# Feed-forward stages of a two-block transformer kernel: one PSUM operand for VectorE's operations of a turn, and the root applied to the up side when it is split

## The chip, the cores and the metric

The kernel runs on one core of a Trainium2 chip. The metric is the device time of one execution in microseconds. Engine names in the profile: PE is TensorE (PEld its weight loads), DVE is VectorE, ACT is ScalarE, POOL is GpSimd, SP is SyncE, which issues the DMAs of the weights.

## The reference, cut to what matters

The program is two blocks of a transformer on 512 tokens of width 1024, in float32. Each block ends in a feed-forward part of hidden width 2816. In the first block:

```python
u = rms_norm(h, norm_ffn_g[l])
g, up = jnp.split(u @ w_gate_up[l], 2, axis=-1)
h = h + (jax.nn.silu(g) * up) @ w_down[l]
```

The second block has the same with other names. `rms_norm` multiplies by `rsqrt(mean(h*h) + 1e-6)`, one number per token, and by a gain. Since that number (the root, `rs` in the kernel) is the same for all columns of a token, the kernel multiplies h by the gain only ahead of the product, and by rs behind it. With G and U for the two products without rs, the hidden value is

```
a = silu(G*rs) * (U*rs) = G*rs * sigmoid(G*rs) * U*rs
```

so rs is applied once ahead of the sigmoid and appears twice in the product.

## The kernel before

**Precision.** TensorE multiplies in a rounded format. Each operand is therefore kept as a high part (a rounded copy, made by ScalarE) and a low part (the operand minus its high part), and each product is three matmuls: high by high, high by low, low by high. The low parts of the weights (`w_lo`, `low_part`, L501) are made by GpSimd, each one a subtraction of 128x1024 elements whose two inputs are in SBUF.

**Weights.** All weights come in one stream of units of 128x1024, in a ring of three slots. For each unit SyncE issues the load, ScalarE makes w_hi (`feed`, L1392) once the load has landed and TensorE is done with the unit three before it, whose slot it takes, GpSimd makes w_lo, and TensorE uses it. SyncE may reload a slot when its w_lo is done.

**The feed-forward stages.** ffn1 and ffn2 have 44 units each, gate and up tiles by turns. Tokens lie along the free dimension, so a hidden tile is 128 (columns) x 512 (tokens). The first units (6 in ffn1, 12 in ffn2) and the last two are plain: one unit is one tile of 24 matmuls (`tile_unit`). Between them are turns of six units (6 turns in ffn1, 5 in ffn2, `fast_turns` and `turn`). In a turn the first two pairs of units (e=0 and e=1) are each computed with seven half products of 12 matmuls in place of eight (Strassen's scheme as Winograd orders it; `seven_products`), and the last two units are plain tiles. The scheme needs sums of the weights: VectorE makes three tiles `s_raw` from a pair of units (`weight_sums`, L2631 to L2634), ScalarE the high part `s_hi` (L1810), GpSimd the low part `s_lo` (L521). `weight_sums(i, 1)` serves pair e=1 of the turn, `weight_sums(i, 3)` pair e=0 of the next turn. It needs similar sums of u (`t_sums`, L2601 to L2607, and `t_low`, L2614), which are made once at the stage's head.

**What VectorE does per turn**, in this order (`ffn_dve`, `turn`): the up tile of the turn before (`plain_up`, L2583); the weight sums of pair 1; `late_sums` (L2641), after which it signals `fast_z`, on which TensorE waits ahead of the pair's seventh product; `late_up` (L2646); `fast_gate` (L2652 to L2657), which completes the gate tile and multiplies it by rs into tmp[1]; ScalarE's sigmoid E of it goes to PSUM bank 3; `fast_up` (L2665 to L2667): E times gate, times rs, times up, into `a_raw`. The same for e=1, with the weight sums of pair 3 ahead of its `fast_up`. Then the plain gate tile (`plain_gate`, L2569), whose sigmoid goes to `e_tmp` in SBUF, and `plain_mid` (L2577, L2578): gate times E, times rs. `step` makes VectorE wait for each operation's own end before the next.

**The order is written out by hand** on each engine; nothing is planned. Each engine works through its program in order, and semaphores tie them.

**The end of a stage.** The high parts a_hi lie where the sums of u and weights were (t_hi, t_lo, s_raw), and a_lo is written in the place of a_raw. So they can be made only behind the last product of the last turn. ScalarE's `split(k)` makes a_hi from a_raw when `fast_a` says tile k is done; VectorE's `split` makes a_lo behind it (L2674). Between them the last gate and up tiles are done. ScalarE feeds the last unit of ffn and the first two of the down stage among its splits; the down stage's third unit and those behind it are fed by `down_act`, behind all 22 splits and a load of the activation table, and in ffn1 also behind the eight squares of `mem_in` (L1412, L1417). From the third on, each of those waits for VectorE's addition (`add_square`, L2194), and these stand behind VectorE's last split. `down` on TensorE (banks 2 to 5 first, then 6, 7, 0, 1) uses two hidden tiles per unit.

Of the kernel before, what the change touches and what calls it, by code (L numbers as in the profile page):

```python
# [116 lines left out]
def build(nc, stream, xT, memT, vecs, tabs, relb, outT):  # L117
    with ExitStack() as ctx, ExitStack() as work:
# [89 lines left out]
        t_raw = [ar(f"t_raw{i}", [P, 4, HALF], F32, 80 + 4 * i) for i in range(2)]  # L208
        first_two = tmp[2]
        late_two = tmp[4]  # L210
        e_tmp = tmp[5]

        bq = ar("bq", [P, 4, T], F32, 0)
        bk = ar("bk", [P, 4, T], F32, 8)
# [102 lines left out]
        def named(n):  # L317
            if n not in nsem:
                nsem[n] = sem(n)
            return nsem[n]  # L320
# [70 lines left out]
        def ffn2_banks(pair):  # L391

            return [(1, 6), (0, 7), (4, 5)][pair]

        FAST = {"ffn1": (FIRST["ffn1"] + 2 * R, 6), "ffn2": (FIRST["ffn2"] + 4 * R, 5)}
        E_BANK = 3

        def out_banks(pair):

# [977 lines left out]
        def _(act):  # L1377
# [398 lines left out]
            def ffn_act(name, first, at_end=None):  # L1776
# [3 lines left out]
                if name == "ffn1":  # L1780
                    act.sem_inc(named("fast_s_used"), 2)

                def gate(dst):

                    gates.use()
                    act.wait_ge(*of_fast(name, "gate", gates.value()))
                    act.activation(dst, tmp[1][:, :], ACT.Sigmoid).then_inc(named("fast_e"), 1)

                def plain_gate():
                    gate(e_tmp[:, :])  # L1790

                def t_tile(k):

# [25 lines left out]
                def split(k):  # L1819

                    act.wait_ge(*of_fast(name, "a", k + 1))
                    act.activation(a_hi[:, k], a_raw[:, k], ACT.Copy).then_inc(named("raw_hi"), 1)

                def turn(i, last):

                    feed_at(i, 2)
                    copy(i, 0)
                    sums_hi(i, 1)
                    feed_at(i, 3)
                    feed_at(i, 4)  # L1830
                    gate(ps[:, E_BANK, :])
                    copy(i, 1)
                    feed_at(i, 5)
                    feed_at(i, 6)
                    gate(ps[:, E_BANK, :])
                    if last:
                        act.wait_ge(*of_fast(name, "s_used", 2 * turns + 2))
                        if at_end:
                            at_end()
                        for k in range(4):  # L1840
                            split(k)
                        feed_at(i, 7)
                        plain_gate()
                        for k in range(4, 8):
                            split(k)
                        feed_at(i, 8)
                        for k in range(8, 12):
                            split(k)
                        feed_at(i, 9)
                        plain_gate()  # L1850
                        for k in range(12, 20):
                            split(k)
                    else:
                        sums_hi(i, 3)
                        feed_at(i, 7)
                        plain_gate()

                first(FIRST[name], plain_gate, t_tile, sums_hi)
                with repeat(act, turns - 1, [(gates, R)]) as i:
                    turn(i, False)  # L1860
                turn(turns - 1, True)
                split(20)
                split(21)
                exponentials()

            def memory_split():
# [314 lines left out]
        def _(dve):  # L2181
# [374 lines left out]
            def ffn_dve(name, gain):  # L2556
# [13 lines left out]
                    dve.sem_inc(bank_free[bank], 1)  # L2570
                    dve.sem_inc(named("fast_gate"), 1)

                def plain_mid():

                    made.use()
                    dve.wait_ge(*of_fast(name, "e", made.value()))
                    step(dve.tensor_tensor(tmp[1][:, :], tmp[1][:, :], e_tmp[:, :], ALU.mult))  # L2577
                    step(dve.tensor_tensor(tmp[1][:, :], tmp[1][:, :], rs[:, :], ALU.mult))  # L2578

                def plain_up(t, bank, k):  # L2580

                    dve.wait_ge(w_used, t + 1)
                    step(dve.tensor_tensor(a_raw[:, bass.ds(k, 1)], ps[:, bank, :].unsqueeze(1), tmp[1][:, :].unsqueeze(1),  # L2583
                                           ALU.mult))
                    dve.sem_inc(bank_free[bank], 1)
                    dve.sem_inc(named("fast_a"), 1)

                def pair(j, banks):

# [47 lines left out]
                def late_sums(i, e):  # L2637

                    dve.wait_ge(*of_fast(name, "prod", i * 4 + (2 * e + 2)))
                    dve.wait_ge(*of_fast(name, "copied", i * 2 + (e + 1)))  # L2640
                    step(dve.tensor_tensor(late_two[:, :], ps[:, ffn2_banks(e)[1], :], first_two[:, :], ALU.add))  # L2641
                    dve.sem_inc(named("fast_z"), 1)

                def late_up():

                    step(dve.tensor_tensor(late_two[:, H], late_two[:, H], late_two[:, L], ALU.add))  # L2646

                def fast_gate(i, e):

                    x, y = ffn2_banks(e)  # L2650
                    dve.wait_ge(*of_fast(name, "s_used", i * 2 + (e + 3)))
                    step(dve.tensor_tensor(tmp[1][:, H], ps[:, y, H], late_two[:, L], ALU.add))  # L2652
                    dve.sem_inc(bank_free[y], 1)
                    step(dve.tensor_tensor(tmp[1][:, L], ps[:, x, L], rs[:, L], ALU.mult))
                    step(dve.tensor_tensor(tmp[1][:, H], tmp[1][:, H], rs[:, H], ALU.mult))  # L2655
                    dve.sem_inc(named("fast_gate"), 1)
                    step(dve.tensor_tensor(late_two[:, L], ps[:, x, H], late_two[:, L], ALU.add))  # L2657
                    dve.sem_inc(bank_free[x], 1)

                def fast_up(k):  # L2660

                    made.use()
                    dve.wait_ge(*of_fast(name, "e", made.value()))
                    x = ps[:, E_BANK, :]
                    step(dve.tensor_tensor(x, x, tmp[1][:, :], ALU.mult))  # L2665
                    step(dve.tensor_tensor(x, x, rs[:, :], ALU.mult))
                    step(dve.tensor_tensor(a_raw[:, bass.ds(k, 1)], x.unsqueeze(1), late_two[:, :].unsqueeze(1), ALU.mult))  # L2667
                    dve.sem_inc(named("fast_a"), 1)

                def split(first, last):  # L2670

                    for k in range(first, last):
                        dve.wait_ge(*of_fast(name, "a_hi", k + 1))
                        step(dve.tensor_tensor(a_lo[:, k], a_raw[:, k], a_hi[:, k].bitcast(F32), ALU.subtract))  # L2674
                        dve.sem_inc(named("raw_lo"), 1)

                def turn(i, last):

# [32 lines left out]
                plain_gate(u - 2, ffn2_banks(2)[0])  # L2711
                plain_mid()

                with repeat(dve, turns - 1, [(own, 30), (made, 3)]) as i:
                    turn(i, False)
                turn(turns - 1, True)
                t = u + turns * 2 * R
                split(0, 2)
                plain_up(t - 1, ffn2_banks(2)[1], FT - 2)
                split(2, 6)  # L2720
                plain_gate(t, ffn2_banks(0)[0])
                split(6, 10)
                plain_mid()
                plain_up(t + 1, ffn2_banks(0)[1], FT - 1)
                split(10, FT)

            def down_ready(name, n):
                if n < 3:
# [451 lines left out]
```

## Time and profile before

| | |
|---|---|
| time, median of 3 runs | 1761.22 us (1760.53 to 1762.3) |
| the profiled execution's own time | 1761.26 us |
| its span (first to last instruction) | 1759.4 us |
| mean granted TensorE clock | 0.99 |
| busy, share of the span | TensorE 96%, VectorE 58%, GpSimd 43%, ScalarE 42% |

The span is 1.9 us shorter than the execution's own time. In the profile a line such as L737 is a line of the kernel before; a group is one line with one kind of operands. "tmp<-ps,tmp" is an operation that writes a tile in SBUF from one in PSUM (ps) and one in SBUF. In brackets stands the engine's idle time ahead of the operation and what ended it; "x2" are two operations in a row shown as one. The clock is a share of full speed. In time, ffn1's turns run from about 442 to 645 us, ffn2's from about 1442 to 1607.

### The profile page before, as it was taken

Reading aid. Unit: us, or ns where it says so; the run is one execution under the profiler, and the core shown is the slowest. Engines: PE = TensorE matmul, PEld = TensorE weight load, DVE = VectorE, ACT = ScalarE, POOL = GpSimd, SP = SyncE. Lnnn points to the kernel's source line nnn. Section 1 sums busy time; section 2 is a strip of 40 time slices with the busy share of each in tenths; the row PEclk is TensorE's granted clock in tenths of the full one; section 3 lists DMA queues with packets and bytes.
Section 4 is the critical chain, followed back from the end, with each engine's and each line's share of the span. In section 5 each row is a group of like instructions: output and inputs, shape, how many; then the busy total and the mean of one; then the engine's idle time right before and its main releaser. Section 6 shows DMA issues by size and latency. Waiting matters only on the chain.

```text
span 1759.4 us, 25747 instructions
## 1 busy us (share of the span) xinstructions
PE 1693.7 (96%) x8873; PEld 1393.2 (79%) x8877; DVE 1017.9 (58%) x1608; ACT 731.9 (42%) x1187; POOL 757.9 (43%) x330
## 2 busy tenths in 40 slices
PE   9999999999889997999999999999999988999999
PEld 7888777787788886888788766778888868888887
DVE  6744875657776674207497676642324886677413
ACT  7333554433333343326434576552233523334322
POOL 2444222444666663354433102544444336656443
PEclk9999999999999998999999999999999989999999
DMA  5444221232222332234422111223323212333332
GB/s 198 130 147 140 95 61 49 84 91 78 85 85 92 97 119 72 82 110 122 145 88 93 41 45 48 61 65 93 105 92 113 72 60 84 97 94 96 96 96 72
DMA packets 47643, 162.37 MB, mean 92 GB/s; under 512 B 5724, under 2 KB 7900, under 8 KB 47304
## 3 DMA queue, kind: packets, MB, share of 16 engines
q1 hardware_dynamic: 43440, 150.70, 27.6%
q10 hardware_dynamic: 4120, 10.59, 1.9%
q8 instruction: 48, 0.79, 0.2%
q14 instruction: 35, 0.29, 0.1%
HBM read 156.91 MB, written 4.76 MB: 92 GB/s over the span
## 4 chain that ended last, share of the span: by engine, by line
PE 73%; DVE 17%; issue 4%; ACT 3%; POOL 2%; DVEq 1%; ACTq 0%; POOLq 0%
PE ps L619 18%; PE ps L621 17%; PE ps L620 17%; DVE tmp L2578 2%; PE ps L737 2%; PE ps L739 2%; PE ps L738 2%; PE ps L877 2%; POOL s_lo L521 2%; PE ps L859 2%; DVE tmp L2577 2%; DVE s_raw L2631 1%; DVE tmp L2655 1%; PE ps L1311 1%; PE ps L1310 1%
## 5 line engine op out<-in xcount | busy, mean ns | idle before, releaser
L501 POOL TENSOR_TENSOR w_lo<-w_raw,w_hi 128x1024 fp32r<-128x1024 f32 x260 | 642.6, 2480 | 764.2 <-ACT w_hi L1392 737.4
L1392 ACT ACTIVATE w_hi<-w_raw 128x1024 fp32r<-128x1024 f32 x271 | 284.1, 1054 | 333.2 <-PE ps L621 223.0
L619 PE MATMUL ps<-u_hi,w_hi 128*128 128x512 f32 x984 | 404.0, 411 | 11.3 <-POOL w_lo L501 11.1
L621 PE MATMUL ps<-u_hi,w_lo 128*128 128x512 f32 x984 | 385.1, 391 | 0.0
L620 PE MATMUL ps<-u_lo,w_hi 128*128 128x512 f32 x984 | 385.0, 391 | 0.0
L619 PEld LDWEIGHTS ps<-u_hi,w_hi 128*128 128x128 f32 x984 | 185.6, 189 | 57.0 <-POOL w_lo L501 12.2
L621 PEld LDWEIGHTS ps<-u_hi,w_lo 128*128 128x128 f32 x984 | 185.4, 188 | 40.0
L620 PEld LDWEIGHTS ps<-u_lo,w_hi 128*128 128x128 f32 x984 | 185.9, 189 | 37.0 <-issue 1.4
L521 POOL TENSOR_TENSOR s_lo<-s_raw,s_hi 128x1536 fp32r<-128x1536 f32 x22 | 77.0, 3500 | 112.8 <-ACT s_hi L1810 112.8
L619 PE MATMUL ps<-a_hi,w_hi 128*128 (+1 forms) x264 | 104.1, 394 | 9.7 <-POOL w_lo L501 9.7
L620 PE MATMUL ps<-a_lo,w_hi 128*128 (+1 forms) x264 | 103.7, 393 | 0.0
L621 PE MATMUL ps<-a_hi,w_lo 128*128 (+1 forms) x264 | 103.5, 392 | 0.0
L1810 ACT ACTIVATE s_hi<-s_raw 128x1536 fp32r<-128x1536 f32 x22 | 32.7, 1488 | 108.7 <-DVEq L2635 108.7
L568 POOL TENSOR_TENSOR masked_bias<-bias,pick 128x128 f32<-128x128 f32 (+3 forms) x32 | 25.5, 824 | 104.5 <-PE ps L1207 103.7
L737 PE MATMUL ps<-t_hi,s_hi 128*128 128x256 f32 x176 | 52.4, 298 | 16.0 <-POOL s_lo L521 16.0
L619 PEld LDWEIGHTS ps<-a_hi,w_hi 128*128 128x128 f32 x264 | 50.1, 190 | 20.5 <-issue 10.1
L2533 DVE TENSOR_TENSOR tmp<-ps,tmp 128x512 f32<-128x512 f32 x16 | 11.1, 691 | 91.1 <-PE ps L621 90.0
L621 PEld LDWEIGHTS ps<-a_hi,w_lo 128*128 128x128 f32 x264 | 50.1, 190 | 10.7
L620 PEld LDWEIGHTS ps<-a_lo,w_hi 128*128 128x128 f32 x264 | 50.1, 190 | 10.5
L619 PE MATMUL ps<-m_hi,w_hi 128*128 128x512 f32 (+1 forms) x152 | 54.3, 357 | 0.0
L620 PE MATMUL ps<-m_lo,w_hi 128*128 128x512 f32 (+1 forms) x152 | 54.0, 356 | 0.0
L621 PE MATMUL ps<-m_hi,w_lo 128*128 128x512 f32 (+1 forms) x152 | 54.0, 356 | 0.0
(456 smaller groups left out, 3647.5 us busy)
## 6 DMA issues: line engine op xcount, KB each, us to landing
w_raw<-stream SPq DMA_DIRECT2D x277, 512.0 KB, 3.5
g_rep<-g_one ACTq DMA_DIRECT2D x1, 2560.0 KB, 13.1
spread<-m_rows ACTq DMA_DIRECT2D x4, 512.0 KB, 4.2
tmp<-tmp ACTq DMA_DIRECT2D x32, 64.0 KB, 3.1
bias<-g_rep ACTq DMA_DIRECT2D x1, 2048.0 KB, 10.6
outT<-hT SPq DMA_DIRECT2D x13, 128.0 KB, 1.8
hT<-xT SPq DMA_DIRECT2D x3, 512.0 KB, 7.4
mem_in<-memT ACTq DMA_DIRECT2D x1, 1024.0 KB, 6.4
```

Source lines behind the costliest of these rows:

```text
L501: pool.tensor_tensor(w_lo[:, slot], w_raw[:, slot], w_hi[:, slot].bitcast(F32), ALU.subtract)\
L521: pool.tensor_tensor(s_lo[pair % 3][:, :, :], s_raw[:, :, :], s_hi[pair % 3][:, :, :].bitcast(F32), ALU.subtract).then_inc(named("raw_lo"), 1)
L619: pe.matmul(out, wh, xh, start=start, stop=False)
L620: pe.matmul(out, wh, xl, start=False, stop=False)
L621: return pe.matmul(out, wl, xh, start=False, stop=stop)
L737: pe.matmul(out, w_h(k), x_h(k), start=start and k == 0, stop=False, skip_group_check=True)
L738: pe.matmul(out, w_h(k), x_l(k), start=False, stop=False, skip_group_check=True)
L739: m = pe.matmul(out, w_l(k), x_h(k), start=False, stop=stop and k == HK - 1, skip_group_check=True)
L859: m = pe.matmul(ps[:, 2 + e, 0:keys[t]], head_q(h, t), head_k(h, keys[t]), start=True, stop=not extra(t))
L877: m = pe.matmul(ps[p0:p1, b, t * P:t * P + P], values(h, kb), prT[e][:, kb * P:kb * P + P], start=kb == 0, stop=kb == nb - 1)
L1392: act.activation(w_hi[:, slot], w_raw[:, slot], ACT.Copy).then_inc(hi_ready, 1)
L2577: step(dve.tensor_tensor(tmp[1][:, :], tmp[1][:, :], e_tmp[:, :], ALU.mult))
```

## The change

Four things change, all in ffn1 and ffn2.

1. **The root of the up side.** `fast_up` and `plain_mid` no longer multiply by rs. `a_raw` is therefore without the second rs, and a new step `rooted` multiplies each of its 22 tiles by rs in place, behind the last turn and ahead of the split. The signal `fast_a`, on which ScalarE's `split` waits, moves from `fast_up` and `plain_up` to `rooted`.
2. **E in PSUM.** The sigmoid of the plain gates goes to PSUM bank 3 as those of the other gates do, the very last one to bank 7; `e_tmp` goes. `plain_mid` is one multiply that reads E from PSUM.
3. **Sums through bank 2.** `late_sums` is split in two halves, one of which goes to bank 2; `fast_gate` puts its half-wide sum in bank 2 in place of tmp[1]. So `late_up` and the multiply of old line 2655 read one operand from PSUM.
4. **The order of the end.** VectorE roots tiles 0 and 1, then 2 to 5, 6 to 9, with the splits a group behind, then root k and split k-2 by turns up to the last. ScalarE has its feeds and gates among the splits in another spacing: feed, gate, splits 0 and 1, feed, splits 2 to 5, feed, gate, splits 6 to 21.

```diff
-        e_tmp = tmp[5]
-        E_BANK = 3
+        C_BANK, E_BANK, LAST_E_BANK = 2, 3, 7
...
-                def gate(dst):
+                def gate(bank=E_BANK):
...
-                    act.activation(dst, tmp[1][:, :], ACT.Sigmoid).then_inc(named("fast_e"), 1)
+                    act.activation(ps[:, bank, :], tmp[1][:, :], ACT.Sigmoid).then_inc(named("fast_e"), 1)
...
                     if last:
                         act.wait_ge(*of_fast(name, "s_used", 2 * turns + 2))
                         if at_end:
                             at_end()
-                        for k in range(4):
-                            split(k)
                         feed_at(i, 7)
-                        plain_gate()
-                        for k in range(4, 8):
+                        gate()
+                        for k in range(2):
                             split(k)
                         feed_at(i, 8)
-                        for k in range(8, 12):
+                        for k in range(2, 6):
                             split(k)
                         feed_at(i, 9)
-                        plain_gate()
-                        for k in range(12, 20):
+                        gate(LAST_E_BANK)
+                        for k in range(6, FT):
                             split(k)
...
-                def plain_mid():
+                def plain_mid(bank=E_BANK):
...
-                    step(dve.tensor_tensor(tmp[1][:, :], tmp[1][:, :], e_tmp[:, :], ALU.mult))
-                    step(dve.tensor_tensor(tmp[1][:, :], tmp[1][:, :], rs[:, :], ALU.mult))
+                    step(dve.tensor_tensor(tmp[1][:, :], ps[:, bank, :], tmp[1][:, :], ALU.mult))
...
-                    step(dve.tensor_tensor(late_two[:, :], ps[:, ffn2_banks(e)[1], :], first_two[:, :], ALU.add))
+                    y = ffn2_banks(e)[1]
+                    step(dve.tensor_tensor(late_two[:, L], ps[:, y, L], first_two[:, L], ALU.add))
+                    step(dve.tensor_tensor(ps[:, C_BANK, H], ps[:, y, H], first_two[:, H], ALU.add))
...
-                    step(dve.tensor_tensor(late_two[:, H], late_two[:, H], late_two[:, L], ALU.add))
+                    step(dve.tensor_tensor(late_two[:, H], ps[:, C_BANK, H], late_two[:, L], ALU.add))
...
-                    step(dve.tensor_tensor(tmp[1][:, H], ps[:, y, H], late_two[:, L], ALU.add))
+                    step(dve.tensor_tensor(ps[:, C_BANK, L], ps[:, y, H], late_two[:, L], ALU.add))
...
-                    step(dve.tensor_tensor(tmp[1][:, H], tmp[1][:, H], rs[:, H], ALU.mult))
+                    step(dve.tensor_tensor(tmp[1][:, H], ps[:, C_BANK, L], rs[:, H], ALU.mult))
...
-                    step(dve.tensor_tensor(x, x, rs[:, :], ALU.mult))
                     step(dve.tensor_tensor(a_raw[:, bass.ds(k, 1)], x.unsqueeze(1), late_two[:, :].unsqueeze(1), ALU.mult))
-                    dve.sem_inc(named("fast_a"), 1)
...
+                def rooted(first, last):
+
+                    for k in range(first, last):
+                        step(dve.tensor_tensor(a_raw[:, k], a_raw[:, k], rs[:, :], ALU.mult))
+                        dve.sem_inc(named("fast_a"), 1)
...
-                split(0, 2)
+                rooted(0, 2)
                 plain_up(t - 1, ffn2_banks(2)[1], FT - 2)
-                split(2, 6)
+                rooted(2, 6)
+                split(0, 4)
                 plain_gate(t, ffn2_banks(0)[0])
-                split(6, 10)
-                plain_mid()
+                rooted(6, 10)
+                plain_mid(LAST_E_BANK)
+                split(4, 8)
                 plain_up(t + 1, ffn2_banks(0)[1], FT - 1)
-                split(10, FT)
+                for k in range(10, FT):
+                    rooted(k, k + 1)
+                    split(k - 2, k - 1)
+                split(FT - 2, FT)
```

## Rows read from the trace of the kernel before

**Rows 1.** The page's busy line: busy us, share of the span, instructions per engine.
```profile
PE 1693.7 (96%) x8873; PEld 1393.2 (79%) x8877; DVE 1017.9 (58%) x1608; ACT 731.9 (42%) x1187; POOL 757.9 (43%) x330
```

**Rows 2.** What TensorE waited for, whole span: total us, times, longest.
```profile
PE ps L619 <- POOL w_lo L501: 20.8, 3, 9.7
...
PE ps L737 <- DVEq L2642: 20.0, 11, 2.0
...
PE ps L737 <- POOL s_lo L521: 16.0, 18, 5.2
```

**Rows 3.** TensorE in time order, ffn1: start, us, line, operation [idle before].
```profile
496.15 0.39 PE L737 MATMUL ps<-t_hi,s_hi 128*128 128x256 f32 x1 [1.10 <-POOL s_lo L521]
...
504.89 0.40 PE L619 MATMUL ps<-u_hi,w_hi 128*128 128x512 f32 x1
...
527.03 0.39 PE L737 MATMUL ps<-u_hi,s_hi 128*128 128x256 f32 x1 [1.96 <-DVEq L2642]
...
531.27 0.39 PE L737 MATMUL ps<-t_hi,s_hi 128*128 128x256 f32 x1 [1.10 <-POOL s_lo L521]
```

**Rows 4.** VectorE's groups by line and shape: busy us, mean ns, idle before.
```profile
L2578 DVE TENSOR_TENSOR tmp<-tmp,tmp 128x512 f32<-128x512 f32 x22 | 42.4, 1927 | 0.8
...
L2655 DVE TENSOR_TENSOR tmp<-tmp,tmp 128x256 f32<-128x256 f32 x22 | 41.1, 1870 | 0.8
...
L2666 DVE TENSOR_TENSOR ps<-ps,tmp 128x512 f32<-128x512 f32 x22 | 15.4, 700 | 0.8
```

**Rows 5.** VectorE in time order, the same turn of ffn1.
```profile
505.09 0.42 DVE L2652 TENSOR_TENSOR tmp<-ps,tmp 128x256 f32<-128x256 f32 x1 [2.96 <-PE ps L739]
505.66 0.42 DVE L2654 TENSOR_TENSOR tmp<-ps,tmp 128x256 f32<-128x256 f32 x1
506.12 2.28 DVE L2655 TENSOR_TENSOR tmp<-tmp,tmp 128x256 f32<-128x256 f32 x1
...
509.35 0.69 DVE L2631 TENSOR_TENSOR s_raw<-w_raw 128x512 f32<-128x512 f32 x1 [0.38 <-DVE tmp L2657]
...
516.50 1.61 DVE L2577 TENSOR_TENSOR tmp<-tmp,tmp 128x512 f32<-128x512 f32 x1 [0.85 <-ACT tmp L1787]
518.14 2.78 DVE L2578 TENSOR_TENSOR tmp<-tmp,tmp 128x512 f32<-128x512 f32 x1
...
521.60 0.69 DVE L2583 TENSOR_TENSOR a_raw<-ps,tmp 128x512 f32 x1 [0.67 <-DVE tmp L2578]
522.79 0.95 DVE L2631 TENSOR_TENSOR s_raw<-w_raw 128x512 f32<-128x512 f32 x1 [0.50 <-DVE a_raw L2583]
```

**Rows 6.** GpSimd in time order, the same turn.
```profile
503.35 4.77 POOL L501 TENSOR_TENSOR w_lo<-w_raw,w_hi 128x1024 fp32r<-128x1024 f32 x2 [2.34 <-ACT w_hi L1392]
...
514.04 3.52 POOL L521 TENSOR_TENSOR s_lo<-s_raw,s_hi 128x1536 fp32r<-128x1536 f32 x1 [5.93 <-ACT s_hi L1810]
...
517.50 5.69 POOL L501 TENSOR_TENSOR w_lo<-w_raw,w_hi 128x1024 fp32r<-128x1024 f32 x2
```

**Rows 7.** End of ffn1: VectorE's last turn and last splits, TensorE's wait.
```profile
645.59 0.42 DVE L2652 TENSOR_TENSOR tmp<-ps,tmp 128x256 f32<-128x256 f32 x1 [3.13 <-PE ps L739]
...
671.16 9.93 DVE L2674 TENSOR_TENSOR a_lo<-a_raw,a_hi 128x512 fp32r<-128x512 f32 x12 [0.25 <-DVE a_raw L2583]
...
687.83 0.79 PE L619 MATMUL ps<-a_hi,w_hi 128*128 x1 [9.69 <-POOL w_lo L501]
```

**Rows 8.** End of ffn2: VectorE's last raw tile, GpSimd's first w_lo behind it.
```profile
1632.01 0.69 DVE L2583 TENSOR_TENSOR a_raw<-ps,tmp 128x512 f32<-128x512 f32 x1
...
1635.98 2.45 POOL L501 TENSOR_TENSOR w_lo<-w_raw,w_hi 128x1024 fp32r<-128x1024 f32 x1 [8.64 <-ACT w_hi L1392]
```

**Rows 9.** Heads of ffn1 and ffn2: TensorE's waits in time order.
```profile
447.43 0.58 PE L737 MATMUL ps<-t_hi,s_hi 128*128 128x256 f32 x1 [5.25 <-POOL s_lo L521]
...
1434.18 0.79 PE L619 MATMUL ps<-u_hi,w_hi 128*128 128x512 f32 x1 [8.38 <-POOL w_lo L501]
```

**Rows 10.** Busy time and granted clock in the window behind ffn1's wait.
```profile
688.00:692.00 4.00, 4.00 (x10) 3.13 (x11) 0.00 (x0) 0.00 (x0) 4.00 (x2) 0.50 0.57 156
```

More of the change, by code:

```diff
@@ L1781, in ffn_act @@
                     act.sem_inc(named("fast_s_used"), 2)
-                def gate(dst):
+                def gate(bank=E_BANK):
                     gates.use()
                     act.wait_ge(*of_fast(name, "gate", gates.value()))
-                    act.activation(dst, tmp[1][:, :], ACT.Sigmoid).then_inc(named("fast_e"), 1)
-                def plain_gate():
-                    gate(e_tmp[:, :])
+                    act.activation(ps[:, bank, :], tmp[1][:, :], ACT.Sigmoid).then_inc(named("fast_e"), 1)
                 def t_tile(k):
@@ L1830, in turn @@
                     feed_at(i, 4)
-                    gate(ps[:, E_BANK, :])
+                    gate()
                     copy(i, 1)
@@ L1834, in turn @@
                     feed_at(i, 6)
-                    gate(ps[:, E_BANK, :])
+                    gate()
                     if last:
@@ L1839, in turn @@
                             at_end()
-                        for k in range(4):
-                            split(k)
                         feed_at(i, 7)
-                        plain_gate()
-                        for k in range(4, 8):
+                        gate()
+                        for k in range(2):
                             split(k)
                         feed_at(i, 8)
-                        for k in range(8, 12):
+                        for k in range(2, 6):
                             split(k)
                         feed_at(i, 9)
-                        plain_gate()
-                        for k in range(12, 20):
+                        gate(LAST_E_BANK)
+                        for k in range(6, FT):
                             split(k)
@@ L1855, in turn @@
                         feed_at(i, 7)
-                        plain_gate()
-                first(FIRST[name], plain_gate, t_tile, sums_hi)
+                        gate()
+                first(FIRST[name], gate, t_tile, sums_hi)
                 with repeat(act, turns - 1, [(gates, R)]) as i:
@@ L1861, in ffn_act @@
                 turn(turns - 1, True)
-                split(20)
-                split(21)
                 exponentials()
@@ L2665, in fast_up @@
                     step(dve.tensor_tensor(x, x, tmp[1][:, :], ALU.mult))
-                    step(dve.tensor_tensor(x, x, rs[:, :], ALU.mult))
                     step(dve.tensor_tensor(a_raw[:, bass.ds(k, 1)], x.unsqueeze(1), late_two[:, :].unsqueeze(1), ALU.mult))
-                    dve.sem_inc(named("fast_a"), 1)
                 def split(first, last):
@@ L2712, in ffn_dve @@
                 plain_mid()
-                with repeat(dve, turns - 1, [(own, 30), (made, 3)]) as i:
+                with repeat(dve, turns - 1, [(own, 29), (made, 3)]) as i:
                     turn(i, False)
```

## The prediction

> **What bounds the kernel now.** I read the page's busy line first, then TensorE's waits, the lines with their shapes, one turn of ffn1 in time order, and last the ends of the stages. TensorE is busy 1693.7 of 1759.4 us [rows 1], so only 65.7 us of idle can be won. Three rows hold 56.8 of them [rows 2]: 20.8 us for a w_lo (three waits), 20.0 for VectorE's `fast_z` (L2642), 16.0 for the s_lo of a weight sum. The last two, both on L737, come back in each of the eleven turns of ffn1 and ffn2: 1.96 and 1.10 us in one turn [rows 3], and 0.23 more for the s_lo of its first sum. The turn lasts 35.12 us (531.27 less the 496.15 of the same product one turn earlier).
>
> VectorE is late in a turn because some of its operations are stretched. With both inputs in SBUF the 512-wide L2578 takes 1927 ns on average and the 256-wide L2655 1870; L2666 (512), which reads PSUM, takes 700 [rows 4], and L2652 (256) 0.42 us. In the turn, L2655 (506.12 to 508.40) can only have worked in its last 0.42 us, from 507.98: GpSimd's pair of w_lo ends at 508.12 [rows 5, 6]. L2577 (its last 0.69 begins at 517.42) comes through as the s_lo ends (517.56), L2578 waits for the first w_lo of the next pair (to 520.23) and L2631 for the second (to 523.05, pair's end 523.19). So a VectorE operation with two SBUF inputs waits for the GpSimd operation under way, until 0.14 us before its recorded end, and then the engines alternate: 0.69 for VectorE, 2.12 for a w_lo.
>
> The Trainium skill ("SBUF — State Buffer", Who interferes with whom) says the same of two SBUF inputs against a GpSimd operation that reads SBUF: whoever issues first holds the port for the whole instruction, the other fully blocks. It speaks against this change in the ends below, whose added operations all have two SBUF inputs. Held for the recorded length, each collision would cost 0.14 us more, about 3 us in the sum; the rows decide for the shorter one.
>
> **A full turn after the change.** I count x from the turn's first plain tile (504.89 [rows 3]). TensorE does two tiles to x=10.92, then products of 1.44 (12 matmuls, 0.12 between starts). VectorE starts at x=0.20.
> Pair 3: L2655 reads PSUM, 0.43 instead of 2.28. L2657 ends at 2.24; the weight sums would start at 2.62 (0.38 gap, as before 509.35), wait for the w_lo pair until 3.1 and end at 5.95 (0.69+3×0.72), before at 7.33. Their s_lo is ready at 11.3; TensorE wants it at 12.36. The wait of 0.23 goes.
> `fast_up` loses L2666 (0.73); the gate L2569 ends at 8.6, the sigmoid at 9.5, the middle multiply (one, from PSUM) at 10.2, where L2578 ended at 16.03. What is late next is TensorE: the up tile ends at 10.92, so L2583 runs 11.3 to 12.0 instead of 16.71 to 17.40 [rows 5].
> Pair 1: its sums could start at 12.5 (0.50 gap), and they keep two SBUF inputs. Behind s_lo GpSimd has two w_lo in a row, 11.25 to 13.5 and on (the second one's w_hi waits for the up tile too, ready at 12.2). L2631 waits to 13.5 and ends at 14.2, L2632 waits to 16.3, the four end at 18.45 (before: 21.02).
> `fast_z`: L2641, now two of 0.43, is done at 19.65. TensorE wants it at 10.92+6×1.44=19.56: 0.2 of the 1.96 stays.
> s_lo of pair 1 comes 5.36 after its sums (from 522.79+0.95+3×0.725 = 525.91 to 531.27 before), 23.8; TensorE, 0.3 late, wants it at 22.75: 1.05 of the 1.10 stays. Six more products: 23.9+8.64=32.55. **A full turn takes 32.55 instead of 35.12, 2.55 us less, nine times (five in ffn1, four in ffn2): 22.9.** That is more than the idle shown, since a stop costs 0.26 beyond it: a matmul's modelled end lies 0.16 behind the next start, and the first one behind a stop takes 0.39, not 0.28.
> In the first turn of each stage both stay late, since its sums of pair 1 meet the same two w_lo: 1.1 less each, 2.2.
>
> **The heads.** ffn1: L2578 (2.85 at one pair, 2.83 at the next) goes; 1.2 is lost again, as the t-sums wait for the w_lo of 421.14 instead, and 1.1 as L2631 meets one. The first product with a sum starts 3.4 earlier than 447.43 [rows 9]. ffn2: four pairs lose 0.72 each ahead of the feed that ends the 8.38 wait of 1434.18 [rows 9], and collisions of its t-sums shift: 2.6 (bounds 0 and 5). Together 6.0.
> Won: 22.9+2.2+6.0 = 31.1 us.
>
> **The ends.** Here work is added: 22 multiplies by rs (`rooted`) per stage behind the last turn, each ahead of ScalarE's a_hi of its tile. No row shows them; the nearest is two SBUF inputs, 512 wide, GpSimd quiet: 0.69 (the last three sums of a turn), plus 0.15 for the increment behind it (L2652 to L2654 in [rows 5] shows that gap): 0.84. A split costs 0.845 likewise.
> I count D from L2652 of the last turn (645.59 [rows 7]). The gate waits for its tile to 5.5; middle done 7.8; root 0 waits for a w_lo, root 1 done 10.4; up waits for its tile (x=11.1, which is D 10.9), done 11.7; root 2 12.55; a w_lo holds root 3 to 14.65; root 5 17.0; splits 0 to 3 with one w_lo 22.5; gate 23.3; roots 6 to 9 26.7; middle 27.55; splits 4 to 7 30.9; up 31.75; then twelve times root and split, 1.69 each. The last root ends at 31.95+11×1.69+0.69 = 51.2, the last split at 53.8, before at 35.5 (681.09, [rows 7]). a_lo itself isn't late: splits 0 and 1 are done at 18.8, down's first unit starts at 21.8; 2 and 3 at 22.5, the second at 27.2.
> What TensorE will lack is weights. ScalarE feeds down's third unit only behind its last `split`, and in ffn1 behind the squares of mem_in too, whose additions stand behind VectorE's last split. TensorE wants that unit at 687.83-9.69-645.59 = D 32.55 [rows 7].
> ffn1: the chain from last split to w_lo is the same, so all of it moves by 53.8-35.5: **18.3**; the 9.69 wait becomes 28.
> ffn2 has no squares. From its last raw tile (1632.70) over a_hi, table load, w_hi and w_lo (to 1635.98+2.4 [rows 8]) are 5.7: 51.2+5.7 = 56.9 against 32.55: **24.4**, where no wait stood. Behind such a wait the granted clock is 0.50, 1.2 GHz [rows 10]; ffn1's end has that already, in ffn2's twelve matmuls are new at 0.43 between starts instead of 0.23: 2.4.
> Nothing gives this back: TensorE has no other long wait in [rows 2] behind either end.
> Cost: 18.3+24.4+2.4 = 45.1. Bounds: with no w_lo in VectorE's way each end is 4.1 shorter, 36.9 in all; with roots at L2578's 1.93 it would be 94, but GpSimd is idle through most of the tail for want of feeds, so I stay near the lower bound. The turn's term lies between 0 and 3.97 (no stop left, 31.15).
>
> **Sum:** 45.1-31.1 = +14.0 us on the profiled execution's 1761.26 (span 1759.4 and 1.9 around it): 1775.3. The median of the runs shown is 1761.22, the same within their spread.
>
> At nothing I put: E in PSUM at plain gates (ScalarE writes beside VectorE's next wait), bank 7 for the last E (free until down's second half), `late_up` and `fast_gate` through bank 2 (same widths, no other user of bank 2 in a turn). Uncovered, they'd cost under 0.1 a turn. No DMA is added; SP's loads follow w_lo and the sums, and at the ends they have long landed when ScalarE comes.
>
> **Rivals.**
> (a) Not slower: VectorE gets the port twice running when a w_lo ends. Then L2631 and L2632 pass together, s_lo comes 2 us earlier, and a turn has no stop. Won 9×3.97+4+6.7 = 46.4; at the ends roots aren't held, 36.9: **1751.8**. If the turns alone have it, **1760.0**. It decides from 4 us won a turn. For: at 509 to 512 four operations follow one another freely; against: L2578 lost the port right behind L2577.
> (b) GpSimd keeps the port through both w_lo: the sums of pair 1 end 0.5 later, turn 33.1, won 2.0 instead of 2.55: **1780**. Against: L2577 got in between.
> (c) It doesn't do what it says, PSUM readers wait too: no gain, 45 lost: **1806**. Against: L2652 and L2654 took 0.42 inside a w_lo.
>
> **Numbers.** Forecast 0.50; (a) in full 0.10, in the turns alone 0.17; (b) 0.20; (c) 0.03. Faster by over 0.2% (3.5 us, about what can be told from no change here): 0.11; within: 0.16; slower: 0.73. The range 1757 to 1781 takes in (b) and (a) in the turns.
>
> **What would show it.** L2655 and the middle multiply at 0.43 and 0.69; turns of 32.6 with a fast_z wait near 0.2 and an s_lo wait near 1; waits for w_lo of 28 us at ffn1's end and 24 at ffn2's; 54 us from L2652 of the last turn to the last split. I am wrong if ffn2's end has no wait over 15 us, or if turns stay over 34 or fall to 31.2.

## The result and the profile after

The changed kernel takes 1774.74 us (median of 4 runs, 1774.49 to 1775.64) where the kernel before, timed beside it, takes 1761.41 (4 runs, 1760.53 to 1762.3): ratio 1.0077, interval 1.0059 to 1.0094. It is slower, by 13.3 us where 14.0 were forecast. Its profiled execution took 1774.81 us, its span 1773.0.

The busy line and TensorE's longest waits of the changed kernel, to be read against [rows 1, 2] (total us, times, longest):

```profile
PE 1688.8 (95%) x8873; PEld 1389.4 (78%) x8877; DVE 987.4 (56%) x1630; ACT 735.9 (42%) x1187; POOL 747.8 (42%) x330
```

```profile
PE ps L618 <- POOL w_lo L500: 58.9, 4, 28.3
PE ps L736 <- POOL s_lo L520: 13.9, 13, 3.5
...
PE ps L736 <- DVEq L2634: 1.0, 1, 1.0
```

Two of the three rows of before have shrunk: the `fast_z` wait from 20.0 us in 11 places to 1.0 in one (ffn2's first turn), the s_lo wait from 16.0 to 13.9. The third, TensorE waiting for a weight's low part, has grown from 20.8 to 58.9. Where it grew, and where a turn stands, are in TensorE's own rows (start, duration, in brackets the idle time ahead):

```profile
444.23 0.58 PE L736 MATMUL ps<-t_hi,s_hi 128*128 128x256 f32 x1 [3.48 <-POOL s_lo L520]
...
489.25 0.39 PE L736 MATMUL ps<-t_hi,s_hi 128*128 128x256 f32 x1 [0.91 <-POOL s_lo L520]
...
497.99 0.40 PE L618 MATMUL ps<-u_hi,w_hi 128*128 128x512 f32 x1
...
517.41 0.28 PE L738 MATMUL ps<-t_hi,w_lo 128*128 128x256 f32 x1
517.76 0.39 PE L736 MATMUL ps<-u_hi,s_hi 128*128 128x256 f32 x1
...
521.81 0.39 PE L736 MATMUL ps<-t_hi,s_hi 128*128 128x256 f32 x1 [0.92 <-POOL s_lo L520]
...
689.16 0.79 PE L618 MATMUL ps<-a_hi,w_hi 128*128 x1 [28.31 <-POOL w_lo L500]
...
1432.87 0.79 PE L618 MATMUL ps<-u_hi,w_hi 128*128 128x512 f32 x1 [5.55 <-POOL w_lo L500]
...
1650.92 0.79 PE L618 MATMUL ps<-a_hi,w_hi 128*128 x1 [24.00 <-POOL w_lo L500]
```

A turn of ffn1 takes 521.81 - 489.25 = 32.56 us (35.12 before), with one listed stop of 0.92 in it. A second, of 0.23, is not in the list of waits: the product that waits for `fast_z` starts 0.35 us behind the matmul before it (517.41 to 517.76) where 0.12 is usual, and that matmul's modelled end hides the gap. The two long waits stand ahead of the third unit of each down stage; [rows 7] have 9.69 there, ffn2 had none.

VectorE's groups, beside [rows 4] (busy us, mean ns of one, idle ahead), and its operations around pair 1's sums, with GpSimd's after them, beside [rows 5, 6]:

```profile
L2622 DVE TENSOR_TENSOR w_raw<-w_raw 128x512 f32<-128x512 f32 x22 | 40.2, 1827 | 0.8
L2621 DVE TENSOR_TENSOR s_raw<-w_raw 128x512 f32<-128x512 f32 x22 | 37.7, 1715 | 9.0 <-DVE a_raw L2574 3.8 <-DVE tmp L2649 3.5 <-POOL s_lo L520 1.7
...
L2647 DVE TENSOR_TENSOR tmp<-ps,tmp 128x256 f32<-128x256 f32 x22 | 9.3, 424 | 0.8
```

```profile
507.34 0.69 DVE L2569 TENSOR_TENSOR tmp<-ps,tmp 128x512 f32<-128x512 f32 x1 [0.83 <-ACT ps L1786]
...
510.33 1.86 DVE L2621 TENSOR_TENSOR s_raw<-w_raw 128x512 f32<-128x512 f32 x1 [0.41 <-DVE a_raw L2574]
512.22 2.77 DVE L2622 TENSOR_TENSOR w_raw<-w_raw 128x512 f32<-128x512 f32 x1
...
515.75 0.69 DVE L2624 TENSOR_TENSOR s_raw<-w_raw,s_raw 128x512 f32<-128x512 f32 x1
...
517.22 0.43 DVE L2633 TENSOR_TENSOR ps<-ps,tmp 128x256 f32<-128x256 f32 x1
```

```profile
509.21 5.23 POOL L500 TENSOR_TENSOR w_lo<-w_raw,w_hi 128x1024 fp32r<-128x1024 f32 x2
518.26 3.50 POOL L520 TENSOR_TENSOR s_lo<-s_raw,s_hi 128x1536 fp32r<-128x1536 f32 x1 [3.82 <-ACT s_hi L1806]
```

The multiply of old line 2655 (now L2647) fell from 1870 to 424 ns. The collisions have not gone, they moved on to the first two weight sums, which still read two SBUF operands: 1715 and 1827 ns, where they took 956 and 785 before. L2621 ends at 512.19, L2622 at 514.99, each behind one w_lo of the GpSimd pair.

The end of ffn1 in the changed kernel: VectorE, then ScalarE, then GpSimd; and ffn2's end, ScalarE:

```profile
628.30 0.43 DVE L2644 TENSOR_TENSOR ps<-ps,tmp 128x256 f32<-128x256 f32 x1 [2.87 <-PE ps L738]
...
678.86 0.69 DVE L2670 TENSOR_TENSOR a_raw<-a_raw,tmp 128x512 f32<-128x512 f32 x1
679.70 2.37 DVE L2664 TENSOR_TENSOR a_lo<-a_raw,a_hi 128x512 fp32r<-128x512 f32 x3
```

```profile
679.64 0.63 ACT L1818 ACTIVATE a_hi<-a_raw 128x512 fp32r<-128x512 f32 x1 [1.05 <-DVEq L2671]
680.29 1.28 ACT L1381 ACT_TABLE_LOAD   x1
...
683.11 2.53 ACT L1416 ACTIVATE tmp<-mem_in 128x256 f32<-128x256 f32 x5 [0.26 <-DVE tmp L2186]
685.55 2.93 ACT L1391 ACTIVATE w_hi<-w_raw 128x1024 fp32r<-128x1024 f32 x3
```

```profile
686.66 6.99 POOL L500 TENSOR_TENSOR w_lo<-w_raw,w_hi 128x1024 fp32r<-128x1024 f32 x3 [37.38 <-ACT w_hi L1391]
```

```profile
1645.35 0.63 ACT L1818 ACTIVATE a_hi<-a_raw 128x512 fp32r<-128x512 f32 x1 [1.04 <-DVEq L2671]
...
1647.29 2.95 ACT L1391 ACTIVATE w_hi<-w_raw 128x1024 fp32r<-128x1024 f32 x3
```

Each a_hi waits 1.05 us for VectorE's signal, so ScalarE moves at VectorE's pace of 1.68 per tile, and the feed of a weight unit that landed long before (the core's DMA queues moved nothing from 655 to 688 us) stands behind it; GpSimd was idle for 37.38 us for want of a w_hi. What TensorE waits for is the weight's low part at the end of that chain, not a hidden tile.

### The profile page after: what moved, and what is told of

The parts are those of the page before. It is cut to its first block, busy times and chain, and to the rows that moved or that the text cites. A ratio compares the mean times of both kernels' runs of the same rounds, so it can differ in the third digit from the quotient of the medians.

```text
span 1773.0 us, 25759 instructions
## 1 busy us (share of the span) xinstructions
PE 1688.8 (95%) x8873; PEld 1389.4 (78%) x8877; DVE 987.4 (56%) x1630; ACT 735.9 (42%) x1187; POOL 747.8 (42%) x330
## 4 chain that ended last, share of the span: by engine, by line
PE 76%; DVE 10%; issue 7%; ACT 4%; POOL 3%; DVEq 0%; DMA 0%; ACTq 0%; POOLq 0%; SPq 0%
PE ps L618 19%; PE ps L619 19%; PE ps L620 19%; POOL s_lo L520 2%; DVE w_raw L2622 2%; PE ps L736 2%; PE ps L738 2%; PE ps L737 2%; PE ps L876 2%; DVE s_raw L2621 2%; PE ps L858 1%; PE ps L1310 1%; PE ps L1309 1%; PE ps L1308 1%; PE ps L902 1%
## 5 line engine op out<-in xcount | busy, mean ns | idle before, releaser
L500 POOL TENSOR_TENSOR w_lo<-w_raw,w_hi 128x1024 fp32r<-128x1024 f32 x260 | 632.6, 2442 | 809.8 <-ACT w_hi L1391 783.0
L619 PEld LDWEIGHTS ps<-u_lo,w_hi 128*128 128x128 f32 x984 | 185.8, 189 | 36.9 <-issue 1.4
L736 PE MATMUL ps<-t_hi,s_hi 128*128 128x256 f32 x176 | 51.8, 295 | 13.9 <-POOL s_lo L520 13.9
```

Of the source, the lines that this page charges most:

```text
L500: pool.tensor_tensor(w_lo[:, slot], w_raw[:, slot], w_hi[:, slot].bitcast(F32), ALU.subtract)\
L619: pe.matmul(out, wh, xl, start=False, stop=False)
L736: pe.matmul(out, w_h(k), x_h(k), start=start and k == 0, stop=False, skip_group_check=True)
```

## The experiments

The theory to be tested: what the turns, heads and new operand places win (31 us) and what the ends lose (45 us) are independent; the win comes from the port shared with GpSimd, the loss from the feeds behind 22 `fast_a` signals that now come late. Times are medians; each is compared with the kernel before (1761.3 to 1761.7 in these runs) with its 95% interval.

**1. The operands alone.** The kernel before with every operation of a turn but the weight sums reading one operand from PSUM, the root back in the turn and the ends as before. Against the changed kernel, the lines of the turn are:

```diff
-                    step(dve.tensor_tensor(tmp[1][:, :], ps[:, bank, :], tmp[1][:, :], ALU.mult))
+                    step(dve.tensor_tensor(ps[:, bank, :], ps[:, bank, :], tmp[1][:, :], ALU.mult))
+                    step(dve.tensor_tensor(tmp[1][:, :], ps[:, bank, :], rs[:, :], ALU.mult))
...
                     step(dve.tensor_tensor(x, x, tmp[1][:, :], ALU.mult))
+                    step(dve.tensor_tensor(x, x, rs[:, :], ALU.mult))
```

> The changed kernel with the root back in the turn: fast_up multiplies E by rs in PSUM as before, the plain middle is two multiplies (E times gate in PSUM, then times rs into tmp[1]), each with one PSUM operand, and the ends of the stages are the old ones. Theory (the turn wins because no operation but the weight sums waits for GpSimd's port, the ends lose because of the 22 roots): the two extra multiplies of 0.73 fall into VectorE's slack ahead of the up tile and behind it the sums of pair 1 wait for the same w_lo, so a turn stays at 32.6 and the ends cost what they did before (9.7 in ffn1, nothing in ffn2): 1761.4 - 31.8 = 1729.6 us (1727 to 1733). Rival 1 (the turn wins because it has three multiplies fewer): turns go back by 2.2 us each, about 1750 or more. Rival 2 (the long waits at the ends come from elsewhere, such as E in PSUM or bank 7): still 24 us at the end of ffn2, about 1770.

Measured: 1730.42 us (1729.82 to 1731.39), ratio 0.9823 [0.9807, 0.9839]. TensorE's longest wait and its rows in this kernel:

```profile
PE ps L618 <- POOL w_lo L500: 18.0, 3, 9.6
```

```profile
521.86 0.39 PE L736 MATMUL ps<-t_hi,s_hi 128*128 128x256 f32 x1 [0.92 <-POOL s_lo L520]
...
554.42 0.39 PE L736 MATMUL ps<-t_hi,s_hi 128*128 128x256 f32 x1 [0.92 <-POOL s_lo L520]
...
670.56 0.79 PE L618 MATMUL ps<-a_hi,w_hi 128*128 x1 [9.60 <-POOL w_lo L500]
```

The turn is 32.56, that of the changed kernel to the hundredth, with the root still in it. So once the operands are in PSUM, taking the root out of a turn wins nothing: what it would save is time in which VectorE waits for TensorE's up tile. The whole win in the turns is that of the operands' places, and the wait at ffn1's end is back at 9.60. The root does count in one place: at ffn2's head TensorE waits 7.40 us for a w_lo here and 5.55 in the changed kernel, 1.85 less, since VectorE has one multiply fewer in each plain pair ahead of that feed.

**2. One multiply back in SBUF.** The changed kernel, but `fast_gate`'s sum and multiply work in tmp[1] as before:

```diff
-                    step(dve.tensor_tensor(ps[:, C_BANK, L], ps[:, y, H], late_two[:, L], ALU.add))
+                    step(dve.tensor_tensor(tmp[1][:, H], ps[:, y, H], late_two[:, L], ALU.add))
...
-                    step(dve.tensor_tensor(tmp[1][:, H], ps[:, C_BANK, L], rs[:, H], ALU.mult))
+                    step(dve.tensor_tensor(tmp[1][:, H], tmp[1][:, H], rs[:, H], ALU.mult))
```

> The changed kernel with one edit undone: the half-wide sum of fast_gate goes to tmp[1] again and its multiply by rs has two SBUF inputs, twice a turn; number and size of the operations are the same. Theory: the one behind pair 1 waits for the pair of w_lo (0.42 becomes about 2.3), the sums of pair 3 end 1.7 later, s_lo misses TensorE by 0.5, everything behind is late too, turn about 34.1 instead of 32.6: 1789 us (1784 to 1793). Rival (fewer operations): no difference, 1775.

Measured: 1787.37 us (1786.76 to 1787.86), ratio 1.0148 [1.0131, 1.0165]. The multiply's group and the `fast_z` wait in this kernel:

```profile
L2647 DVE TENSOR_TENSOR tmp<-tmp,tmp 128x256 f32<-128x256 f32 x22 | 40.9, 1860 | 0.8
```

```profile
PE ps L736 <- DVEq L2634: 9.6, 10, 1.0
```

One operand of one 256-wide multiply, twice a turn, is worth 12.6 us (1787.4 less 1774.7): with it in SBUF the operation takes 1860 ns again, `fast_z` is 0.97 late again, and the turn is 557.91 - 523.97 = 33.94.

**3. No roots.** The changed kernel without the 22 multiplies of a stage, so the second rs is missing from the hidden tiles; all signals are kept in their new places:

```diff
-                        step(dve.tensor_tensor(a_raw[:, k], a_raw[:, k], rs[:, :], ALU.mult))
```

> The changed kernel with the 22 multiplies of rooted left out in each stage (the hidden tiles lack their second rs), signals kept. Theory: VectorE's tail is 22 x 0.84 = 18.5 us shorter; the wait at the end of ffn1 is 28 - 18.5 = 9.5 us, at the end of ffn2 below 3 us; turns stay at 32.6: 1730 us (1727 to 1734). Rival (ScalarE's new spacing of feeds and splits makes the waits): both long waits stay within 5 us of 28 and 24, about 1770.

Measured: 1740.27 us (1739.38 to 1740.89), ratio 0.988 [0.9864, 0.9897]. This missed the expectation by 10 us, and it is the most telling of the runs. TensorE's and ScalarE's rows in this kernel:

```profile
671.84 0.79 PE L618 MATMUL ps<-a_hi,w_hi 128*128 x1 [11.35 <-POOL w_lo L500]
...
1615.88 0.79 PE L618 MATMUL ps<-a_hi,w_hi 128*128 x1 [7.41 <-POOL w_lo L500]
```

```profile
661.39 0.63 ACT L1818 ACTIVATE a_hi<-a_raw 128x512 fp32r<-128x512 f32 x1 [0.30 <-DVEq L2670]
662.32 0.63 ACT L1818 ACTIVATE a_hi<-a_raw 128x512 fp32r<-128x512 f32 x1 [0.30 <-DVEq L2670]
```

Without one root multiply ScalarE still waits 0.30 us for each signal: `fast_a` now stands between VectorE's splits, one every 0.93 us. Before, all 22 tiles were signalled once VectorE's last raw tile was written (L2583 at 1632.01 [rows 8]), with twelve splits still to do, and no a_hi waited for those. Of the loss at the ends, 1774.7 - 1740.3 = 34 us are the roots' (17.0 at ffn1 and 16.6 at ffn2 by the waits). The rest is that of the new order, VectorE's and ScalarE's together: against experiment 1 with its old ends it costs 1.75 at ffn1 (11.35 less 9.60), 7.41 at ffn2, and some 2.4 by the slow clock behind that stop (granted 0.50, 1.2 GHz, from 1616 to 1620), in all 11.6. The medians are only 1740.3 - 1730.4 = 10 apart because this kernel waits 2.2 us less at ffn2's head (5.20 for 7.40).

**4. A small low part.** The kernel before, in which GpSimd makes 32 of 1024 columns of each w_lo of the turns and leaves out the others:

```diff
-                    low_part(c % R, i * (2 * R) + (c + 1))
+                    slot = c % R
+                    pool.wait_ge(hi_ready, i * (2 * R) + (c + 1))
+                    pool.tensor_tensor(w_lo[:, slot, 0:32], w_raw[:, slot, 0:32], w_hi[:, slot, 0:32].bitcast(F32), ALU.subtract)\
+                        .then_inc(lo_ready, 1)
```

> The kernel before, with GpSimd's w_lo of the units within the turns cut from 1024 to 32 columns (the low part of those weights is left out but for these), s_lo unchanged. Theory (VectorE is late because it waits for w_lo on the shared port): L2655 falls to 0.42, L2578 to 0.69, no stop of fast_z or s_lo is left, a turn takes 31.15 instead of 35.12: 1720 us (1714 to 1726). Rival (VectorE has too many operations in a turn): its work is the same, the turn stays near 35 us and the time within 5 us of 1761.

Measured: 1720.59 us (1718.98 to 1721.12), ratio 0.9766 [0.9749, 0.9782]. The two multiplies of [rows 4] whose operands both lie in SBUF, in this kernel:

```profile
L2581 DVE TENSOR_TENSOR tmp<-tmp,tmp 128x512 f32<-128x512 f32 x22 | 19.5, 886 | 0.8
...
L2658 DVE TENSOR_TENSOR tmp<-tmp,tmp 128x256 f32<-128x256 f32 x22 | 10.6, 480 | 0.8
```

Not a word of VectorE's program differs from before, and its 256-wide multiply falls from 1870 to 480 ns; the turn takes 553.14 - 522.08 = 31.06 and has no `fast_z` wait. What stretches these two operations is GpSimd's w_lo and nothing of VectorE's own. The multiply ahead of them (old L2577), which meets s_lo, keeps 1317 of its 1458 ns, s_lo being whole.

**5. The deferral alone.** The kernel before with the root taken out of the turn, `rooted`, and the new ends, all operands left in SBUF as they were:

```diff
-                    step(dve.tensor_tensor(tmp[1][:, :], tmp[1][:, :], rs[:, :], ALU.mult))
...
-                    step(dve.tensor_tensor(x, x, rs[:, :], ALU.mult))
...
```

> The kernel before with the deferral of the root alone: L2578, L2666 and the signals moved as in the change, rooted and the new order of the ends, but the sum of fast_gate, the sum of late_sums and E of the plain gates stay in SBUF. Theory: in a turn L2655 still waits 1.9 for the w_lo pair and the middle multiply for s_lo; the turn is about 34.3 instead of 35.12 (0.8 x 9 plus some 5 in the heads and first turns = 12 won), the ends cost 45: 1761.6 - 12 + 45 = 1794 us (1789 to 1799). Rival (the gain in the turn comes from the removed multiplies, not from the PSUM operands): turn 32.6, 1775.

Measured: 1791.91 us (1790.71 to 1792.66), ratio 1.0168 [1.0151, 1.0185]. The turn is 559.64 - 525.27 = 34.37, the long waits are there (59.5 us for w_lo in four). With experiment 1 this splits the change: the operands alone -31.2, the deferral alone +30.3, both together +13.3. The parts add up to -0.9, 14.2 less than the whole, so the two are not independent. Alone, the deferral wins 35.12 - 34.37 = 0.75 in each of nine full turns, 3.8 at ffn1's head (first sum product at 443.66 against 447.43) and 3.1 at ffn2's (the wait for w_lo is 5.31 there against 8.38), 13.6 in all. Once these operations read PSUM, only some 1.8 of that is left, at ffn2's head (experiment 1). That accounts for 11.8 of the 14.2; the rest was not traced.

**6. Roots first.** The changed kernel with the last 12 roots together, ahead of the last 14 splits:

```diff
-                for k in range(10, FT):
-                    rooted(k, k + 1)
-                    split(k - 2, k - 1)
-                split(FT - 2, FT)
+                rooted(10, FT)
+                split(8, FT)
```

> The changed kernel with the last twelve roots in a row ahead of the last fourteen splits, in place of root and split by turns. Theory: the last root ends 11 x 0.845 = 9.3 us earlier, and in ffn2 ScalarE's last a_hi and the feed behind it with it: wait 24.0 - 9.3 = 14.7 us; ffn1's stays at 28.3, because there the feed stands behind VectorE's last split: 1774.7 - 9.3 = 1765.4 us (1763 to 1768). Rival (the total of VectorE's tail counts in both): 1775.

Measured: 1764.9 us (10 runs, 1763.26 to 1765.69), ratio 1.0018 [1.0008, 1.0027], inside the 0.2% taken here as no change; but 9.8 less than the changed kernel. ffn1's wait keeps 28.0 us (the squares' additions still stand behind VectorE's last split), ffn2's falls from 24.0 to 14.8, where the signals alone decide. The same operations in another order: 10 us.

**7. The feeds among the splits.** The changed kernel; ScalarE feeds the down stage behind its splits 9, 10, 13, 16, 19 and 21, and two more ahead of the squares:

```diff
                         for k in range(6, FT):
                             split(k)
+                            if k in (9, 10, 13, 16, 19):
+                                feed_after(d + [9, 10, 13, 16, 19].index(k))
...
+                feed_after(d + 5)
                 exponentials()
+                if name == "ffn1":
+                    feed_after(d + 6)
+                    feed_after(d + 7)
...
```

> The changed kernel with ScalarE's feeds of the down stage put among its last splits: the third to seventh unit behind the splits of tiles 9, 10, 13, 16 and 19, the eighth behind the last, in ffn1 two more ahead of the squares of mem_in. VectorE's work is the same. Theory (the long waits are the feed standing behind the last split and the squares, not the hidden tiles being late): both waits go, with their slow clock, 24.0 + 28.3 + 2 x 2.4 = 57 us: 1718 us (1715 to 1724), although VectorE meets some six more w_lo in each tail. Rival (the tiles a_lo are what TensorE would lack next): at a pace of 1.7 us a tile against TensorE's 2.7 they hold only if w_lo do not stop them; if they do, a new wait of 5 to 15 us for VectorE, 1725 to 1745.

Measured: 1730.1 us (1729.94 to 1730.67), ratio 0.982 [0.9804, 0.9837]. The long waits are gone, and 45 us with them, with no VectorE instruction changed; but the size was missed by 12, and the time lies in the range of the rival, by which the hidden tiles are late. It is not they: all eight waits at the ends, 10.4 us together, are for a w_lo, none for VectorE. TensorE's waits at ffn1's end in this kernel:

```profile
666.77 0.49 PE L618 MATMUL ps<-a_hi,w_hi 128*128 x1 [1.06 <-POOL w_lo L500]
...
681.13 0.49 PE L618 MATMUL ps<-a_hi,w_hi 128*128 x1 [1.44 <-POOL w_lo L500]
...
688.31 0.50 PE L618 MATMUL ps<-a_hi,w_hi 128*128 x1 [1.43 <-POOL w_lo L500]
```

A feed comes once in three tiles, and three tiles take VectorE 7.18 us (688.31 - 681.13): three pairs of root and split at 1.68 and 2.15 for one w_lo that holds them up. TensorE needs a unit every 24 x 0.23 = 5.5 us.

**8. A feed every two tiles.** The same with the feeds behind splits 9, 10, 12, 14, 16 and 18, the next one behind the table load. Against the kernel of experiment 7:

```diff
-                            if k in (9, 10, 13, 16, 19):
-                                feed_after(d + [9, 10, 13, 16, 19].index(k))
+                            if k in (9, 10, 12, 14, 16, 18):
+                                feed_after(d + [9, 10, 12, 14, 16, 18].index(k))
...
```

> As the kernel with the feeds among the splits (1730.1 us), but the feeds stand behind the splits of tiles 9, 10, 12, 14, 16 and 18, one per two tiles instead of one per three. Theory (in that kernel each feed had to wait for three roots and splits at 1.68 us and one w_lo that holds VectorE 2.15 us, a beat of 7.18 us against TensorE's 5.45 a unit, hence four waits of 1.1 to 1.5 us per end): a beat of two tiles is 2 x 1.68 + 2.15 = 5.5 us, the waits for w_lo at the ends go, eight times 1.4 + 0.3 = 13 us: 1718 us (1716 to 1722). Rival (the hidden tiles are what is late): 1726 or more.

Measured: 1730.15 us (1728.78 to 1730.35), ratio 0.9824 [0.9807, 0.984], a miss again, and again in the rival's range, though no wait is for a hidden tile. GpSimd and TensorE at ffn1's end, and TensorE at ffn2's:

```profile
681.40 2.39 POOL L500 TENSOR_TENSOR w_lo<-w_raw,w_hi 128x1024 fp32r<-128x1024 f32 x1 [3.14 <-ACT w_hi L1391]
686.93 2.39 POOL L500 TENSOR_TENSOR w_lo<-w_raw,w_hi 128x1024 fp32r<-128x1024 f32 x1 [3.14 <-ACT w_hi L1391]
695.56 4.87 POOL L500 TENSOR_TENSOR w_lo<-w_raw,w_hi 128x1024 fp32r<-128x1024 f32 x2 [6.23 <-ACT w_hi L1391]
```

```profile
667.33 0.49 PE L618 MATMUL ps<-a_hi,w_hi 128*128 x1 [1.06 <-POOL w_lo L500]
...
698.05 0.49 PE L618 MATMUL ps<-a_hi,w_hi 128*128 x1 [2.81 <-POOL w_lo L500]
...
1638.19 0.49 PE L618 MATMUL ps<-a_hi,w_hi 128*128 x1 [2.84 <-POOL w_lo L500]
```

The beat did become 5.53 us (686.93 - 681.40), as expected, and the short waits went but for the first of each end (1.06 and 0.69); but the denser feeds push VectorE's tail back (more w_lo in it), and the one unit fed behind the last split and the table load comes 2.8 late at either end. The two placements lose the same time in different places. Whether another one loses none was not tried.

**9. Operands and feeds.** Experiment 1's kernel, no deferral, with two down feeds among the splits and the others behind them, ahead of the squares:

```diff
+                            if k in (13, 19):
+                                feed_after(d + [13, 19].index(k))
...
+                for m in range(2, 6):
+                    feed_after(d + m)
```

> The kernel with the root in the turn and one PSUM operand throughout (the first experiment, 1730.4 us), with ScalarE's feeds of the down stage among and right behind its last splits, ahead of the squares of mem_in. Theory: of its long waits the 9.6 us at the end of ffn1 goes, with its slow clock of 2.4: 1718.4 us (1716 to 1722). Rival: the wait is given back later, since the squares and the norm of mem_in now come later, and the stage that needs them waits: 1725 or more.

Measured: 1718.53 us (1718.27 to 1718.76), ratio 0.9754 [0.9738, 0.9771], the fastest of all and 56 us under the changed kernel. TensorE has no wait left at either end; of its two waits for a w_lo one is that of ffn2's head (7.4 us), the other, of 1.0, stands in a stage ahead of ffn1:

```profile
PE ps L618 <- POOL w_lo L500: 8.4, 2, 7.4
```

The windows over the two ends (columns: stretch, its length, busy us of PE, PEld, DVE, ACT and POOL, granted clock, DMA share, GB/s):

```profile
640.00:700.00 60.00, 60.00 (x267) 49.69 (x266) 28.01 (x31) 23.49 (x35) 27.21 (x12) 1.00 0.32 94
1575.00:1635.00 60.00, 60.00 (x266) 49.69 (x266) 24.91 (x25) 20.88 (x27) 26.95 (x11) 1.00 0.30 98
```

## Why the prediction was right

**The turn.** Predicted 32.55, measured 32.56, and its inner times hold. Counted from the turn's first plain tile (497.99), pair 1's first sum ends at 14.20 (14.2 predicted), the second at 17.0 (17.0), the four at 18.45 (18.45), the late sums at 19.66 (19.65), s_lo at 23.77 (23.8). It rests on one reading of [rows 5, 6]: a VectorE operation with two SBUF inputs waits for the GpSimd operation under way and then gets in between two w_lo. Rival (a), that it passes twice, would have L2622 at 0.69; it took 2.77. Rival (b), that GpSimd keeps the port through both, would have L2621 wait for the pair; it ended at 512.19, the pair at 514.44. Rival (c) falls with 424 ns for L2647, and experiment 2 puts a price on it. The 0.2 of `fast_z` is there too, as the 0.23 between 517.41 and 517.76; only the list of waits, where the prediction looked for it, doesn't show it.

The Trainium skill ("SBUF — State Buffer", Who interferes with whom) calls the port shared by the two engines an exclusive lock. The traces agree as to which operations meet it (1860 ns with both inputs in SBUF, 424 with one in PSUM, 480 with GpSimd's work cut); that a held operation starts 0.14 us ahead of the GpSimd operation's recorded end stays this case's measurement.

**The heads.** ffn1's first product with a sum starts at 444.23, 3.2 earlier than [rows 9] (3.4 predicted). ffn2's wait fell from 8.38 to 5.55, 2.8 (2.6 predicted). Full turns, first turns and heads together won 31.6 by the rows: 17.3 up to ffn1's last turn (645.59 less 628.30, [rows 7]), 14.3 from the wait at ffn1's end to ffn2's last turn (919.53 before, from 687.83 to 1607.36, less 905.22, from 689.16 to 1594.38). Predicted: 31.1.

**The ends.** From 628.30 to the last split 53.8 us (53.8 predicted), to the last root 51.25 (51.2). The third unit was wanted at 689.16 - 28.31 = 660.85, which is 32.55 behind L2644, the predicted value; the waits are 28.31 and 24.00 (28 and 24 predicted). ffn1's end cost 18.6 (18.3), since its third unit starts 1.3 later than before although the stage began its last turn 17.3 earlier; ffn2's 24.0 and 2.4 of slow clock. Together 45.0 (45.1 predicted). The prediction's upper bound of 94 does not come out of its own terms: 44 roots, each longer by 1.93 - 0.69 = 1.24, add 54.6 to 36.9, which is 91.5. Nothing else hangs on it, and the 44 roots took 0.83 on average.

**Where the sum hid an error.** 45.0 less 31.6 is 13.4, and 13.3 to 13.6 were measured. But the text put the cost of the ends down to one thing, the 22 multiplies at 0.84. The walk in which they stood also carried the new order of the signals, which the text never priced by itself; I then expected experiment 3 to be 10 us faster than it was. It is 34 us of multiplies and, by the waits of experiment 3, 11.6 of order. The total was right because the walk counted every step, not because the cause it named was the whole. Likewise "2.55 less per turn" was told along the changed steps, the root's among them: experiment 1 shows the root's share of it to be nothing once the operands read PSUM.

**What stays open.** Experiments 7 and 8 leave the deferral 11.6 us behind experiment 9. The waits for w_lo account for 8.5 us of it in experiment 7 and 5.5 in 8 (10.4 and 7.4 at the ends, less the 1.9 won at ffn2's head). In 8 the slow clock adds 1.7; at the prediction's 0.26 a stop, the stops' own cost is an estimated 2 us in 7 and 1 in 8. Some 1 and 3 us are then unexplained. That it can't be brought to nothing is argued, from VectorE's full tail, not shown.

## What to carry to other kernels

An operation with both inputs in SBUF beside busy GpSimd can cost several times its length (1870 ns for 424 here, 128x256, with GpSimd busy 43% of the span); if one input can pass through PSUM, try that first, and count which operation inherits the collision. Work moved out of a loop to a stage's end is not free because the loop's engine had time: ask what the next stage's feeds stand behind on each in-order engine, and walk the signals, not only the operations. Leave out the added work alone (experiment 3) to see whether its length or its place costs.

## What the runs showed of the hardware that was not expected

The granted clock does not follow from the length of a stop alone. In experiment 8's kernel TensorE stopped for 2.81 us at 695.2 and for 2.84 at 1635.4. Ahead of both it had run for 15 us without a listed stop at a granted clock of 1.00 (67 matmuls in each stretch, 680 to 695 and 1620 to 1635). The stretches behind them:

```profile
698.10:702.00 3.90, 3.90 (x17) 3.23 (x18) 3.48 (x5) 1.44 (x4) 2.33 (x1) 1.00 0.62 153
...
1638.20:1642.00 3.80, 3.80 (x10) 3.02 (x11) 0.00 (x0) 0.00 (x0) 3.80 (x2) 0.55 0.60 152
```

The first kept 1.00 (2.4 GHz), the second fell to 0.55, mostly the 1.2 GHz level, and cost (1 - 0.55) x 3.8 = 1.7 us more. This is one execution, and what decided between the two is not shown. Short stops have their own price too: in the kernel of experiment 7 a wait of 1.43 us raises the first matmul behind it from 0.39 to 0.49 us.
